# Reordering both openings of a hybrid attention and mixture-of-experts layer: the first tiles of the projection, and the indices and gathers of expert 0

## The chip, the cores and the metric

One core of a Trainium2 chip runs the whole layer as one program. The metric is the device time of one execution in microseconds. Of several executions the median is taken, and it can tell two versions of this kernel apart from about 0.2% (4.5 us) on.

## The reference

```python
h   = rmsnorm(x) @ w_in            # 1024 tokens x 1024 -> 3584 columns, float32
mix = concat(retention(h), stick_breaking_attention(h))
x   = x + mix @ w_out
xf  = rmsnorm(x)
logits = xf @ w_router + b_router            # 32 experts
top_logits, top_idx = lax.top_k(logits, 4)
top_w = softmax(top_logits)
# tokens are sorted by expert; each expert takes its own tokens
gu   = xb @ w_gate_up[e] + b_gate_up[e]      # gate and up, 2 x 1024 columns
hid  = (clip(up) + 1) * min(gate) * sigmoid(1.702 * gate)
y    = hid @ w_down[e] + b_down[e]
x    = x + sum over the 4 experts of y * weight
```

## The kernel before

The program gives each engine one instruction stream of its own, and the streams are tied by counting semaphores that the source writes out: `then_inc` raises one, `wait_ge` holds the engine's queue until it has a value. Within an engine everything runs in the written order.

**The first opening** (to the first product of the input projection). SyncE issues the first four token tiles of x (128 rows each, L506), and behind the second tile seven small vector loads (`load_vectors`, L491 to L496: the norm weights). Then come the first slab of w_in (256 columns, L501), the rope table (L511) and the second slab. ScalarE's queue issues the table of constants (L633, 666 KB), GpSimd's the router's bias and weights (L558, L559). For each tile ScalarE squares and sums (`square`, L638), takes the root (L640); VectorE inverts (L1178) and scales (L1182, `normalise`); TensorE transposes by the identity matrix in the constants (`turn_tile`, L838); VectorE multiplies by the norm weight while it takes the result out of PSUM (L1190, `to_raw`). VectorE does not begin tile 1 until the vectors are in and turned (L1206, L845). A float32 product is made of three faster ones, so each operand is split in an upper part (ScalarE, L644 for weights, L651 for tokens) and a lower part (VectorE subtracts, L1196 for a slab, L1201 for tokens). The first product (L860) needs the lower part of slab 0 and of the first two token blocks.

**The middle** is projection, retention, stick-breaking attention (L942 to L971) and the output projection with the router. There the loop at L1029 does, for tile i, `out_proj(i)` (L1005 to L1007), then `turn(i-1)` (L1018, eight transposes) and `route(i-2)` (L1026). VectorE adds the residual (L1362), ScalarE squares, roots and scales (L762, L764, L769); `turn` waits for the scaled row (`e_norm`), VectorE multiplies by the norm weight into xfT (L1375), and `best` (L1381 to L1392) picks the four experts. Output rows and scaled rows are stored by SyncE (L532, L534).

**The second opening** (from the last router product to the first product of expert 0) is one VectorE chain. `step` makes each instruction wait for the one before. It makes the softmax weights (L1427 to L1430), three bfloat16 parts of them per expert (L1432 to L1438), the position of each token in each expert's list from the rank sums that TensorE makes (L1440 to L1447), and then the list of expert 0: `list_hot` (L1453 to L1460) compares positions with 384 slots in one instruction, TensorE sums (`token_list`, L1053), `list_out` (L1465 to L1469) writes the indices. GpSimd gathers the rows (`gather`, L579 and twice L582), TensorE turns them (L1060, L1064), VectorE takes them out (`tokens_out`, L1474, L1482). Beside that, ScalarE and VectorE split the down bias (L779 to L784, L1514), VectorE clears `hid` (L1503), SyncE loads the 8 MB of expert 0's gate and up weights (L537, four chunks). Then VectorE builds a table of all list entries in 17 chained steps (`table`, L1524 to L1544), and ScalarE waits for all of it (L820) before its first sigmoid.

**The experts.** For each of 32 experts TensorE does eight blocks f of gate and up (L1119), then the down product in two halves (L1099). Block f waits until VectorE has read block f-2 out of PSUM. VectorE does per block L1567, L1569, `hidden_low` (L1556) of the block before, L1575, L1577; at f=1 the next expert's `list_hot`, at f=3 to 6 `lower` (L1551: the lower parts of the down weights), at f=4 `list_out`. The down product waits per block for the lower part of `hid` (`h_lo`) and of the weights (`c_lo`). The three streams of an expert are `block_dve` (L1558), `block_act` (L805) and `block_matmuls` (L1111).

```python
def turn(i):                       # L1011
    e.wait_ge(e_norm, i + 1)
def project(g):                    # L846
    e.wait_ge(ws_lo, u["slab"] + 1)
e.wait_ge(l_hot, 1)                # L1067
token_list()
```

## Time and profile before

| | us |
|---|---|
| median of 3 executions | 2245.34 (2244.52 to 2245.95) |
| the profiled execution's own time | 2247.83 |
| its span, first to last instruction | 2246.0 |
| TensorE busy in the span | 2148.1 (96%) |
| VectorE, ScalarE, GpSimd busy | 1282.2, 765.2, 330.6 |
| HBM traffic | 226 GB/s over the span |

The profiled execution is 2.5 us above the median, and 1.8 us of its time lie outside the span. In rows, times count from the span's start; "PE" is TensorE's products, "PEld" its weight loads, DVE VectorE, ACT ScalarE, POOL GpSimd, SP SyncE; a "q" behind a name is that engine's queue. A float32 product or its weight load in the experts shows as two records.

### The profile page before, as it was taken

The numbers are of one execution on the slowest core, as the hardware profiler recorded it, in microseconds if no ns is written. First come the engines' busy times: TensorE is split into PE (matmuls) and PEld (weight loads), VectorE is DVE, ScalarE is ACT, GpSimd is POOL, SyncE is SP. The second block draws the span as 40 slices with busy tenths as digits, with TensorE's granted clock in tenths as the row PEclk, the third lists the DMA queues.
The fourth block names the chain that finished last, engine by engine and source line by source line (L and its number), as shares of the span: only waits on it lengthen the run. The fifth ranks groups of instructions, "written<-read, shape, count | busy, mean of one in ns | idle before, by whom it ended". The sixth has DMA issues, their size and how long they took to land.

```text
span 2246.0 us, 41668 instructions
## 1 busy us (share of the span) xinstructions
PE 2148.1 (96%) x16349; PEld 1929.3 (86%) x16350; DVE 1282.2 (57%) x2579; ACT 765.2 (34%) x1360; POOL 330.6 (15%) x237
## 2 busy tenths in 40 slices
PE   6999999899969999999999999999999999999996
PEld 5888888677858999899989998999899998999996
DVE  6434534786356565456656654665566665566654
ACT  3243133576113333233333332332333333333332
POOL 1100200200000211112112111111121211212111
PEclk9999999999969999999999999999999999999998
DMA  5231221304365888678979887887798897899983
GB/s 171 79 103 57 94 94 38 113 2 151 113 213 182 287 303 309 221 247 312 324 256 314 310 296 251 289 303 254 268 315 310 309 311 255 283 313 334 331 275 95
DMA packets 257670, 510.12 MB, mean 227 GB/s; under 512 B 7450, under 2 KB 44366, under 8 KB 257294
## 3 DMA queue, kind: packets, MB, share of 16 engines
q1 hardware_dynamic: 234268, 451.96, 56.7%
q0 software_dynamic: 21968, 51.67, 9.4%
q10 hardware_dynamic: 1344, 5.14, 0.7%
q8 instruction: 75, 1.23, 0.2%
q14 instruction: 15, 0.12, 0.0%
HBM read 473.09 MB, written 33.55 MB: 226 GB/s over the span
## 4 chain that ended last, share of the span: by engine, by line
PE 93%; issue 2%; DVE 2%; DMA 1%; POOL 0%; ACT 0%; SPq 0%; ACTq 0%; DVEq 0%; POOLq 0%
PE bank L1119 45%; PE bank L1099 16%; PE bank L860 13%; PE bank L1107 3%; PE bank L958 2%; PE bank L971 2%; PE bank L1005 1%; PE bank L1006 1%; PE bank L1007 1%; PE bank L1060 1%; PE bank L1053 1%; PE bank L942 1%; PE bank L1026 1%; PE bank L1064 1%; PE bank L1084 1%
## 5 line engine op out<-in xcount | busy, mean ns | idle before, releaser
L1119 PE MATMUL bank<-hx,ring 128*128 128x140 f32 (+1 forms) x8192 | 1035.3, 289 | 21.2 <-issue 18.8
L1119 PEld LDWEIGHTS bank<-hx,ring 128*128 128x128 f32 x8192 | 1027.4, 198 | 26.0 <-issue 21.0
L1099 PE MATMUL bank<-work_r,hx_r 128*128 128x512 f32 x1024 | 335.2, 408 | 0.0
L1551 DVE TENSOR_TENSOR mix_r<-ring,work_r 128x1024 fp32r<-128x1024 f32 x256 | 305.1, 1223 | 41.1 <-ACT work_r L792 41.0
L809 ACT ACTIVATE hx<-hx 128x168 f32<-128x168 f32 x256 | 87.9, 344 | 616.1 <-DVE hx L1567 615.0
L1567 DVE TENSOR_SCALAR hx<-bank,small 128x168 f32<-128x168 f32 x256 | 100.4, 392 | 307.7 <-PE bank L1119 307.5
L792 ACT ACTIVATE work_r<-ring 128x1024 fp32r<-128x1024 f32 x256 | 257.7, 1042 | 0.0
L1099 PEld LDWEIGHTS bank<-work_r,hx_r 128*128 128x128 f32 x1024 | 188.2, 189 | 43.8 <-issue 10.4
L1099 PE MATMUL bank<-mix_r,hx_r 128*128 128x512 f32 x512 | 200.0, 391 | 0.0
L800 ACT ACTIVATE hx<-bank,small 128x512 f32<-128x512 f32 x64 | 44.0, 688 | 314.6 <-PE bank L1064 167.9
L603 POOL DMA_INDIRECT out_x<-hx,small x32 | 51.9, 1622 | 658.6 <-ACT hx L802 639.6
L579 POOL DMA_INDIRECT hx<-xn_scratch,small x33 | 33.3, 1009 | 618.7 <-DVE small L1469 618.7
L860 PE MATMUL bank<-hx_r,mix_r 128*128 128x512 f32 x480 | 114.1, 396 | 7.6 <-DVE hx_r L1201 7.6
L815 ACT ACTIVATE hx_r<-hx 128x128 fp32r<-128x128 f32 x256 | 79.0, 308 | 109.7 <-DVE hx L1577 109.7
L860 PEld LDWEIGHTS bank<-hx_r,mix_r 128*128 128x128 f32 x480 | 90.7, 190 | 27.8 <-issue 9.1
L1099 PEld LDWEIGHTS bank<-mix_r,hx_r 128*128 128x128 f32 x512 | 96.1, 188 | 21.0
L860 PE MATMUL bank<-hx_r,work_r 128*128 128x512 f32 x480 | 113.7, 394 | 0.0
L1460 DVE TENSOR_TENSOR work<-hx,cst 128x3072 bf16<-128x3072 f32 x33 | 110.6, 3352 | 0.0
L860 PEld LDWEIGHTS bank<-hx_r,work_r 128*128 128x128 f32 x480 | 89.7, 188 | 20.2 <-issue 1.9
L606 POOL DMA_INDIRECT out_x<-hx,small x64 | 100.4, 1570 | 19.5 <-issue 19.5
L1569 DVE TENSOR_SCALAR hx<-bank,small 128x168 f32<-128x168 f32 x256 | 98.2, 384 | 0.0
L1474 DVE TENSOR_TENSOR hx<-bank,small 128x512 f32<-128x512 f32 x66 | 42.6, 686 | 85.9 <-PE bank L1060 85.9
(220 smaller groups left out, 2335.6 us busy)
## 6 DMA issues: line engine op xcount, KB each, us to landing
ring<-in_w_gate_up SPq DMA_DIRECT2D x128, 2048.0 KB, 12.7
ring<-in_w_down SPq DMA_DIRECT2D x64, 2048.0 KB, 13.8
mix<-in_w_in SPq DMA_DIRECT2D x14, 1024.0 KB, 5.1
work<-in_w_in SPq DMA_DIRECT2D x14, 1024.0 KB, 5.1
ring<-in_x SPq DMA_DIRECT2D x8, 512.0 KB, 8.9
hx<-in_w_out SPq DMA_DIRECT2D x1, 4096.0 KB, 14.7
work<-in_x ACTq DMA_DIRECT2D x8, 512.0 KB, 4.7
out_x<-work SPq DMA_DIRECT2D x8, 512.0 KB, 4.4
```

The source lines that it names most:

```text
L606: e.indirect_dma_start(out=out_quarters, in_=y_o[:, r], in_offset=None, compute_op=ALU.add, out_offset=bass.IndirectOffsetOnAxis(ap=idx_sc ...
L792: e.activation(dn_hi[:, nh, k:k + 2], dn_ring[:, k:k + 2, nh * CH:(nh + 1) * CH], ACT.Copy).then_inc(c_hi, 1)
L809: e.activation(sg[:, f % 2], g1[:, f % 2], ACT.Sigmoid, scale=GALPHA).then_inc(m_sig, 1)
L815: e.activation(hid_hi[:, f], hid[:, f, 0:P], ACT.Copy).then_inc(h_hi, 1)
L860: mm = e.matmul(dst, lhs, rhs, start=k == 0 and (xs is x_hi and ws is w_hi), stop=k == KD - 1 and ws is w_lo)
L1099: mm = e.matmul(bank[2 + t][:, :], h[:, k], w[:, t, k], start=False, stop=k == KD - 1 and w is dn_lo, skip_group_check=True)
L1107: e.matmul(bank[7][quarter_rows(j), r * 2 * P:(r + 1) * 2 * P], hid[:, k, P + r * OV:P + (r + 1) * OV], dn_ring[:, k, j * 2 * P:(j + 1) * ...
L1119: mm = e.matmul(bank[f % 2][:, part * CAP:part * CAP + w], gu_ring[:, k, f * 256 + part:(f + 1) * 256:2], xT[:, k, 0:w], start=k == 0, sto ...
L1460: e.tensor_tensor(hot, pos_s.unsqueeze(2).to_broadcast([P, NT, NH * P]), slot_at.unsqueeze(1).to_broadcast([P, NT, NH * P]), ALU.is_equal) ...
L1551: e.tensor_tensor(dn_lo[:, nh, k:k + 2], dn_ring[:, k:k + 2, nh * CH:(nh + 1) * CH], dn_hi[:, nh, k:k + 2].bitcast(F32), ALU.subtract).the ...
L1567: e.tensor_scalar(g1[:, b], bank[b][:, 0:CAP], be[:, f:f + 1], GLIM, ALU.add, ALU.min)\
L1569: e.tensor_scalar(u1[:, b], bank[b][:, CAP:2 * CAP], be[:, 8 + f:9 + f], GLIM + 1.0, ALU.add, ALU.min).then_inc(m_up, 1)
```

## The change

In the first opening:

- The constants are cut: the identity (128 columns) goes first, the rest follows behind `square(1)` under the semaphore `rest_in`. The seven vectors move from SyncE's queue to ScalarE's. The router's bias and weights are issued once four tiles are squared.
- ScalarE splits slab 0 ahead of `square(3)`; the lower part of slab 0 is made by GpSimd, behind the router's loads, under a semaphore `ws_lo0` for which the first product waits.
- VectorE normalises tile 1 ahead of its wait for the vectors. TensorE turns the vectors ahead of tile 0.

In the router: `turn` transposes the unscaled row as soon as the residual is added, and `best` multiplies the sums by the inverse root in its first instruction.

In the second opening: the positions of expert 0 alone are worked out first, the compare is cut in three (`first_hot`), and two sums (`first_rows`) give the main and the overflow indices with a semaphore each (`p_idx`). The softmax weights and their parts, the positions of the other experts and the biases follow. SyncE holds chunks 2 and 3 of the gate and up weights until the gathers have landed. GpSimd clears `hid` and makes the two subtractions of the down bias, behind the gathers. The 17 table steps go between the blocks of expert 0, which becomes a copy of the VectorE block of its own, as does the last expert.

```diff
@@ sync
-                if i == 1:
-                    load_vectors()
@@
             for c in range(4):
+                if c == 2:
+                    e.wait_ge(g_in, 48)
                 e.dma_start(gu_ring[:, :, c * 512:(c + 1) * 512], gu_r[0, c]).then_inc(gu_in[c], 16)
@@ gpsimd
+            e.wait_ge(a_sq, HT)
             e.dma_start(brt, b_router.to_broadcast([P, NE])).then_inc(rt_in, 16)
             e.dma_start(wr, w_router[0].rearrange("(k p) n -> p k n", p=P)).then_inc(rt_in, 16)
+            e.wait_ge(ws_hi, 1)
+            e.tensor_tensor(w_lo[0], w_raw[0], w_hi[0].bitcast(F32), ALU.subtract).then_inc(ws_lo0, 1)
@@
-            e.wait_ge(l_ok, 1)
-            e.wait_ge(e_st[0], 128)
-            e.wait_ge(e_st[1], 128)
             e.wait_ge(e_prj, 16)
-            gather()
+            e.memset(hid, 0.0).then_inc(h_zero, 1)
+            e.wait_ge(p_idx, 1)
+            gather_main()
+            e.wait_ge(p_idx, 2)
+            gather_over()
+            e.wait_ge(g_in, 48)
+            for g in range(1, 3):
+                e.wait_ge(b_cast, g)
+                rows = slice(0, 3 * NE) if g == 1 else slice(2 * NE, 3 * NE)
+                e.tensor_tensor(b_raw[rows], b_raw[rows], bias_d[rows], ALU.subtract).then_inc(b_sub, 1)
@@ scalar
-            e.dma_start(cst[:, :], consts).then_inc(const_in, 16)
+            e.dma_start(cst[:, 0:P], consts[:, 0:P]).then_inc(const_in, 16)
+            load_vectors()
...
             for i in range(HT):
+                if i == HT - 1:
+                    upper_slab(0)
                 square(i)
-            upper_slab(0)
+                if i == 1:
+                    e.dma_start(cst[:, P:], consts[:, P:]).then_inc(rest_in, 16)
...
             e.wait_ge(sc_done, 48)
+            e.wait_ge(f_step, F_SPREAD)
             e.activation(bias_d, b_raw, ACT.Copy).then_inc(b_cast, 1)
...
-            e.wait_ge(it_step, IT_STEPS)
             with e.Fori(0, NE) as n:
                 block_act(n)
+            e.wait_ge(it_step, IT_STEPS)
@@ tensor
             def turn(i):
-                e.wait_ge(e_norm, i + 1)
+                e.wait_ge(e_x2, 2 * i + 2)
...
-            e.wait_ge(l_hot, 1)
-            token_list()
+            def first_rows(h, dst):
+                for i in range(NT):
+                    mm = e.matmul(dst, hot[:, i, h * P:(h + 1) * P], tw_s[:, i, 0:2], start=i == 0, stop=i == NT - 1)
+                return mm
+
+            e.wait_ge(p_hot, 1)
+            first_rows(0, bank[7][:, 0:2]).then_inc(p_list, 1)
+            e.wait_ge(p_hot, NH)
+            for r in range(RO):
+                mm = first_rows(1 + r, bank[6][:, 2 * r:2 * r + 2])
+            mm.then_inc(p_list, 1)
...
             mm.then_inc(bias_tr, 1)
-            e.wait_ge(bias_ok, 3)
+            e.wait_ge(l_hot, 1)
+            token_list()
             e.wait_ge(g_in, 48)
             turn_tokens()
@@ vector
-            for i in range(1, HT):
+            for i in range(2, HT):
+                to_raw(i - 2)
                 normalise(i)
-                to_raw(i - 1)
-            lower_slab(0)
+            to_raw(HT - 2)
             to_raw(HT - 1)
@@
+            step(e.tensor_scalar(f_n, f_m, -1.0, 1.0, ALU.mult, ALU.add))
+            e.tensor_copy(tw_s[:, :, 0], tile_at)
+            e.tensor_copy(tw_s[:, :, 1], tok_id[:, 0:1].to_broadcast([P, NT]))
...
+            e.wait_ge(f_rank, 1)
+            step(e.tensor_copy(f_cnt, bank[3][:, 0:NE]))
+            step(e.tensor_scalar(pos_t, tok_id, f_cnt[:, 0:1], None, ALU.add))
+            step(e.scalar_tensor_tensor(pos_t, rank[:, :, 0], -2.0, pos_t, ALU.mult, ALU.add))
+            step(e.tensor_tensor(pos_t, pos_t, f_n[:, :, 0], ALU.mult))
+            step(e.tensor_tensor(pos_s, rank[:, :, 0], pos_t, ALU.add))
+            first_hot(0)
+            first_hot(1)
+            e.wait_ge(p_list, 1)
+            step(e.tensor_reduce(l_raw[:, 0:1], bank[7][:, 0:2], X, ALU.add))
+            e.tensor_copy(idx[:, 0:1], l_raw[:, 0:1]).then_inc(p_idx, 1)
+            first_hot(2)
+            e.wait_ge(p_list, 2)
+            step(e.tensor_reduce(l_raw[:, 1:NH], bank[6][:, 0:2 * RO].rearrange("p (r c) -> p r c", c=2), X, ALU.add))
+            e.tensor_scalar(idx[:, 1:NH], l_raw[:, 1:NH], float(GR), quarter, ALU.mult, ALU.add).then_inc(p_idx, 1)
...
-            e.memset(hid, 0.0)
...
+                    if opening:
+                        table_part(f)
...
-            with e.Fori(0, NE) as n:
-                block_dve(n, n)
+            e.wait_ge(h_zero, 1)
+            block_dve(0, 0, 1, True)
+            with e.Fori(1, NE - 1) as n:
+                block_dve(n, n, n + 1)
+            block_dve(NE - 1, NE - 1)
```

## Rows read from the trace of the kernel before

**Rows 1.** The page: the chain that ended last, by engine.

```profile
PE 93%; issue 2%; DVE 2%; DMA 1%; POOL 0%; ACT 0%; SPq 0%; ACTq 0%; DVEq 0%; POOLq 0%
```

**Rows 2.** Two stretches: length, busy PE, PEld, DVE, ACT, POOL, then clock, DMA share, GB/s.

```profile
637.00:637.50 0.50, 0.50 (x3) 0.50 (x4) 0.44 (x3) 0.50 (x1) 0.00 (x0) 0.50 0.00 0
...
660.00:700.00 40.00, 30.60 (x259) 29.87 (x260) 32.70 (x66) 10.34 (x17) 3.88 (x3) 0.78 0.48 167
```

**Rows 3.** The chain of work that ended last, first opening: start, length, what.

```profile
3.89 8.11 DMA small<-in_sb_k_norm_g
...
26.07 7.26 PE bank L860 x24
```

**Rows 4.** Timeline, first opening: start, length, engine, line, tiles, [idle before <- releaser].

```profile
6.25 1.06 ACT L638 ACTIVATE ring<-ring 128x1024 f32<-128x1024 f32 x1 [3.79 <-DMA ring<-in_x]
...
11.28 1.06 ACT L638 ACTIVATE ring<-ring 128x1024 f32<-128x1024 f32 x1 [2.37 <-DMA ring<-in_x]
...
17.91 1.90 ACT L644 ACTIVATE mix_r<-mix 128x2048 fp32r<-128x2048 f32 x1
...
24.70 4.63 DVE L1201 TENSOR_TENSOR hx_r<-ring,hx_r 128x1024 fp32r<-128x1024 f32 x4 [1.12 <-ACT hx_r L651]
```

**Rows 5.** DMA issues of the first 45 us: KB each, us to landing.

```profile
small<-in_w_router POOLq DMA_DIRECT2D x1, 128.0 KB, 9.4
```

**Rows 6.** Timeline: GpSimd and VectorE side by side, first opening and attention.

```profile
35.37 2.28 DVE L1196 TENSOR_TENSOR work_r<-work,work_r 128x2048 fp32r<-128x2048 f32 x1
35.54 3.27 POOL L564 TENSOR_TENSOR ring<-ring,work 128x512 f32<-128x512 f32 x1 [32.51 <-DVE ring L1284]
...
41.56 1.30 POOL L564 TENSOR_TENSOR ring<-ring,work 128x512 f32<-128x512 f32 x1 [2.75 <-DVE ring L1284]
...
403.25 1.90 DVE L1331 TENSOR_TENSOR_SCAN work<-work,ring 128x128 f32<-128x128 f32 x4 [0.29 <-ACT work L722]
...
408.99 12.27 POOL L576 TENSOR_TENSOR ring<-ring 128x512 f32<-128x512 f32 x8 [6.12 <-DMA ring<-ring]
...
413.54 2.28 DVE L1331 TENSOR_TENSOR_SCAN work<-work,ring 128x128 f32<-128x128 f32 x2 [4.10 <-ACT work L722]
```

**Rows 7.** Line L564: all that carries it (min/median/max ns, first and last start).

```profile
L564 POOLq MODIFY_POOL_CONFIG  x2: 68/70/73, 3.0 to 3.0; - x2
```

**Rows 8.** Timeline, end of the router.

```profile
635.56 1.29 DVE L1375 TENSOR_TENSOR work<-bank,small 128x512 f32<-128x512 f32 x2
...
636.88 1.93 PE L1018 MATMUL bank<-cst,work 128*128 128x128 f32 x8 [1.19 <-DVE work L1375]
...
642.44 3.59 PE L1026 MATMUL bank<-small,work 128*128 128x32 f32 x16 [0.38 <-DVE small L1381]
```

**Rows 9.** Timeline, second opening.

```profile
648.31 0.19 DVE L1427 TENSOR_REDUCE work<-work 128x8 f32<-128x32 f32 x1 [0.36 <-ACT work L771]
...
650.25 1.88 DVE L1432 TENSOR_REDUCE work<-work 128x256 f32<-128x1024 f32 x1
...
658.47 3.35 DVE L1460 TENSOR_TENSOR work<-hx,cst 128x3072 bf16<-128x3072 f32 x1
...
663.49 1.02 POOL L579 DMA_INDIRECT hx<-xn_scratch,small  x1 [15.60 <-DVE small L1469]
...
669.95 1.94 PE L1060 MATMUL bank<-cst,hx 128*128 128x128 f32 x8 [5.21 <-DMA hx<-xn_scratch,small]
...
673.57 10.01 PE L1119 MATMUL bank<-hx,ring 128*128 128x140 f32 x64 [0.82 <-DVE hx L1482]
```

**Rows 10.** Timeline, expert 0.

```profile
683.31 1.28 ACT L809 ACT_TABLE_LOAD   x1 [11.67 <-DVE hx L1544]
...
685.06 7.90 PE L1119 MATMUL bank<-hx,ring 128*128 128x140 f32 x64 [1.48 <-DVE hx L1569]
...
701.33 0.39 DVE L1567 TENSOR_SCALAR hx<-bank,small 128x168 f32<-128x168 f32 x1
...
714.47 0.82 PE L1099 MATMUL bank<-work_r,hx_r 128*128 128x512 f32 x2
```

161 lines of the change are left out of this document (92 added, 69 removed).

## The prediction

> **What bounds the kernel now.** The page's chain first: 93% of it is TensorE [rows 1], so most of the kernel can't be moved by this change, and only the two stretches where TensorE waits for other engines count. The windows show the second of them, with 30.6 us of products in 40 at a mean clock of 0.78 [rows 2]. Then the chain in order of time. In the first opening it runs over the last of seven small vector loads, 8.1 us from its issue to its landing at 12.0, and from there over four token tiles and a slab to the first product at 26.07 [rows 3]. x tile 0 is there at 6.25, tile 1 not before 11.28 [rows 4], about when the router's weights land (issued at 2.03, plus 9.4) [rows 5]. In the second opening the chain is VectorE's from the last router product (642.44 plus 3.6) [rows 8] to the index of expert 0, then the gathers from 663.49, TensorE's turns at 669.95 and the first expert product at 673.57 [rows 9]. Past that TensorE stands until 685.06, since VectorE was building the table (ScalarE waited 11.67 us for it) [rows 10].
>
> A gain of 4.5 us (0.2%) is about what the measurement can tell from none.
>
> **First opening, part by part.** *Loads.* Without constants, vectors and router weights in front, tile 0 has the engines to itself. It landed at 6.25 while it shared them with the constants; I take 4.7 and tile 1 before 8. ScalarE's queue now issues eight small loads first, at the 0.3 to 0.4 us that SyncE took for one, so it is free at 3.7, loads its table (1.3) and squares at 5.0: 1.2 earlier than now. The vectors' last issue is at 3.7. Their landing isn't known: no sooner than about 2 us later (5.7), no later than the 8.1 of now (11.8) [rows 3]; I take 8 to 9, since they no longer queue behind a tile. TensorE turns them ahead of tile 0, and up to 9.9 that costs nothing, since VectorE normalises tile 1 meanwhile. At the bound of 11.8 the chain is 1.9 us later.
>
> *The tiles.* Tile 0 is turned from 8.8 on. VectorE takes it out at 10.9 and then needs 2.5 us per tile as now. ScalarE's slab copy (1.90) [rows 4] stands ahead of `square(3)`: 12.55 to 14.45, then `square(3)` to 15.65, for which VectorE waits about 1 us. Tile 3 is out at 19.9, ScalarE's first token copy at 20.9. The slab's subtraction on VectorE, 2.28 [rows 6], is gone from this chain.
>
> *The slab on GpSimd.* This decides the rest. It waits for the fourth square (15.65), issues both router loads (1.8), and starts at 17.5. A subtraction of 128x512 takes it 1.3 us beside a VectorE instruction that reads PSUM, so 128x2048 takes 5.2: done at 22.7. But both engines hold each other up when VectorE reads two operands from SBUF. A GpSimd instruction that began 0.17 behind such a one took 3.27 in place of 1.30; and two VectorE scans took 2.28 while GpSimd was working, where four took 1.90 before [rows 6]. So the token subtraction (1.16 each) [rows 4] that could start at 21.0 waits until 22.7, ends at 23.9, and the first product starts at 24.0. **Gain 2.1 us.** The bounds of the GpSimd instruction are 4.2 (nothing shared, a nearby kind of it took 1.04 for 512) and 13.1 (all four parts as slow as 3.27): first product at 23.0 or 30.8, a gain of 3.1 or a loss of 4.7. I take 5.2, as VectorE reads PSUM in that stretch. The Trainium skill (GPSIMD Engine Reference, Key points) says that the two share their SBUF interfaces and contend when a VectorE instruction has two SBUF inputs; the trace agrees with its 3.27.
>
> Everything behind this point is bound by TensorE and moves with it; the rest of the constants (600 KB) and slab 1 still land before 25.
>
> **The router.** For the last tile `turn` no longer waits for ScalarE's scaled row, at 636.83. But it also waits for PSUM that VectorE empties in L1375 until 636.85 [rows 8]; half the bank is free at 636.2. So only four of eight transposes come 0.6 earlier. **Gain 0.5**, and nothing in the tiles before, where TensorE has the output projection to do. The four waits that are put elsewhere (`e_tr` now ahead of the residual) are met long before. Scaling in `best` replaces an addition at the same length.
>
> **Second opening.** *Indices first.* From the last `best` at 647.7: weights' first step and f_n 0.5, two copies 0.3, rank sums at 649.2, five short steps 1.2 (650.4). The compare of 384 slots takes 3.35 [rows 9], a third of it 1.12: two thirds end at 652.7, the main index is there at 653.0, the third third at 654.2, the overflow indices at 655.3. The main gather goes out at 653.3 instead of 663.49, the two others at 655.6 and 656.9; the last takes up to 1.9 on GpSimd and lands 2 later, as now, near 660.3. *Then the rest,* VectorE alone: 1.9 to the weighted table (648.31 to 650.25). The 8.2 us from there to the compare at 658.47 [rows 9] are 4.3 for three parts of the weights, 0.4 for the copied ranks, 0.3 for f_n, 2.0 for the positions and 1.2 for expert 0's list. So 655.3 + 1.9 + 4.3 + 0.2 for a copy gives 661.6, and TensorE sums by 662.6 and can turn at once, as the gathers are there. VectorE goes on: 2.0 for the other positions, 0.4, biases 1.2, weights of expert 0 0.3: 665.5. It takes the turned tokens out in 2.0 and the first product of expert 0 starts at 667.7, not 673.57: **gain 5.9**. The bound is now VectorE, and the gathers have over 2 us to spare. Chunks 2 and 3 of the weights, held until 660.4, take the 11 us that 4 MB took before and land at about 672.5; block 4 needs them near 686. That edit costs nothing; were the gathers 13 us late it would.
>
> *What is given back.* GpSimd's bias subtraction (96x1024, 2.1 to 2.6 us at its own rate) starts when the gathers land, 660.3, in the middle of VectorE's subtractions of the weight parts, all from SBUF. By the same rows as above VectorE stands still for it: 0 if it falls on reads of PSUM, 2.6 if whole; I take **1.7 lost**. The second one falls on PSUM reads and is free. ScalarE's bias copies end near 671, before its first sigmoid at 673. Clearing `hid` (1.34 on VectorE) is done at 650 in GpSimd's idle time.
>
> *The table inside expert 0.* Its 17 steps are 9.8 us of VectorE (673.3 to 683.1). Now nothing of TensorE waits behind all of them: the stand before 685.06 (1.5) goes. But VectorE has little room. A block is 3.85 us of TensorE [rows 10]; VectorE's own part is 1.75, with a `lower` 2.98 (701.33 on). With table parts of 2.05, 1.02, 1.68, 2.05 and 1.96 blocks 2 to 6 need 3.7, 5.1, 5.3, 4.9 and 4.8, and block 1 has the compare with 4.0 before them. From a first product at S, VectorE starts block 2 at S+15.8 and block 7 at S+39.6, where TensorE has finished it at S+34.6. The down product then waits for the last `hid` parts and ends its first half at S+42.9. Now it begins the second half at 714.47 [rows 10], S+40.9. **So 2.1 are lost again**; between 0 (TensorE finds all it needs) and the whole 9.8.
>
> **The sum.** 2.1 + 0.5 + 5.9 - 1.7 - 2.1 = 4.7 us. The profiled execution would take 2243.1 instead of 2247.83, its span 2241.3; against the median of 2245.34 that is **2240.6 us**. Behind expert 0 TensorE sets the pace. The two further copies of VectorE's block are new code, but VectorE idles several us at the start of each expert: 0.
>
> **Rivals.** *A: the clock survives the router.* The granted clock is at half (1.2 GHz) from 637.0 on [rows 2], and was at full (2.4 GHz) before it, over 1.2 us of idle TensorE behind small products. The last `turn` took 1.93 and the router sums 3.5 each [rows 8], where at full clock the same take 1.04 and 1.9. The new order halves this pause. If the clock holds, 0.9 and twice 1.6 come on top: 2236.5. Against it: the work before the fall is small products in both. 15%.
>
> *B: GpSimd's subtraction holds up the first product,* and the result is slower. For it: 3.27 beside VectorE. At 13.1 us the first product starts at 30.8, 4.7 later than now, and with 2.6 from the middle the time is 2247.4. It decides from 8.5 us on (17.5 to 26.0). A configuration instruction belongs to this line's first use, at 3.0, and there the first arithmetic came 32 us later [rows 7], so what it costs was hidden, and now it would stand on the path. The Trainium skill (GPSIMD Engine Reference, Instruction dispatch) gives some 6 us for the first call of a freshly loaded kernel; by that the first product starts near 28.6 and the time would be about 2245.2. No row shows such a load. 15%.
>
> *C: VectorE stays the bound and the middle gives nothing.* Table and contention at 6.5 together cancel the 6.4 of router and indices; only the first opening's 2.1 is left: 2243.2. 15%.
>
> *D: the edits are hidden anyway,* as with late vectors (0.2 left of the first opening) and gathers slow behind weights: 2245. 5%.
>
> **Chances.** The forecast's case has 50%, with its own range 2238.5 to 2243, a little over half of it beyond 0.2%. Faster 0.28 + 0.15 + some from C = 0.45; slower by over 0.2% only from B with more behind it, 0.08; same 0.47. The range from 2235.0 to 2247.0 holds A, C and D, the ends of the GpSimd term short of its worst, and most of B.
>
> **What would show it.** First L860 near 24.0 with GpSimd's new instruction at 5.2 us ending before it. The last L1018 from near 636.3, at half clock. First gather 10 us earlier than now, landed before the sums of expert 0's weights end. The first L1119 5 us earlier. VectorE busy without a gap from block 1 to 7 of expert 0, and TensorE waiting 2 to 3 us for L1556's output. The forecast is wrong if GpSimd's subtraction exceeds 8.5 us, or if the down product of expert 0 starts its second half less than 1 us earlier than now relative to the first projection product.

## The result and the profile after

The changed kernel takes 2232.18 us (median of 4 runs, 2229.66 to 2237.12) beside 2244.93 us (median of 4 runs, 2242.77 to 2245.95) for the kernel before: a ratio of 0.9942, 95% interval 0.9926 to 0.9957. That is 12.8 us off, where 4.7 were forecast; the time lies below the range's lower end of 2235.0, on the side that had a chance of 0.45. Twice more, on other chips, the same pair gave 0.9936 (0.992 to 0.9951) and 0.9954 (0.9941 to 0.9968). The profiled execution is the longest of the four, 2237.12 us with a span of 2235.3, against a span of 2246.0 before: 10.7 us are to be found in the two traces.

**First opening.** The timeline of the changed kernel answers to the L1196, L1201 and L860 of [rows 3, 4] (start, length, engine, line, tiles, idle before and what ended it):

```profile
17.70 4.51 POOL L560 TENSOR_TENSOR mix_r<-mix,mix_r 128x2048 fp32r<-128x2048 f32 x1
...
20.34 6.36 DVE L1238 TENSOR_TENSOR hx_r<-ring,hx_r 128x1024 fp32r<-128x1024 f32 x4 [1.12 <-ACT hx_r L670]
...
23.45 2.90 PE L885 MATMUL bank<-hx_r,mix_r 128*128 128x512 f32 x6 [4.95 <-DVE hx_r L1238]
```

GpSimd's slab subtraction, the new L560, takes 4.51 us from 17.70 on. The first projection product comes at 23.45 us instead of 26.07. VectorE's four token subtractions, which begin beside GpSimd, take 6.36 us together where they took 4.63. The first product needs only the first of them (two token blocks). That one takes 2.96 us where the others take 1.21, and ends at 23.30, 1.1 us behind GpSimd's end at 22.21 (min/median/max ns of the line):

```profile
L1238 DVE TENSOR_TENSOR hx_r<-ring,hx_r x4: 1212/1213/2956, 20.3 to 25.5; 128x1024 fp32r<-128x1024 f32 x4
```

**This lead does not last in the profiled execution.** At the half turn of the projection TensorE waits 2.56 us in both kernels. Here are the 48 products behind that wait, first before, then after:

```profile
218.03 11.16 PE L860 MATMUL bank<-hx_r,mix_r 128*128 128x512 f32 x48 [2.56 <-DVE hx_r L1201]
```

```profile
216.43 12.77 PE L885 MATMUL bank<-hx_r,mix_r 128*128 128x512 f32 x48 [2.56 <-DVE hx_r L1238]
```

They take 11.16 us before and 12.77 after. The windows put this down to the granted clock, the column ahead of the last two: from 210 to 230 us it is 1.00 before and 0.91 after.

```profile
210.00:230.00 20.00, 17.44 (x99) 1.00 0.16 53
```

```profile
210.00:230.00 20.00, 17.45 (x86) 0.91 0.16 53
636.00:660.00 24.00, 12.89 (x96) 0.52 0.79 257
660.00:700.00 40.00, 33.05 (x286) 0.82 0.66 229
```

The clock from 636 to 660 us is near half level (1.2 GHz), as it was before, and from 660 to 700 us TensorE has 33.1 us of products in the place of 30.6 [rows 2].

**Second opening.** The rows that answer to those of [rows 8, 9], all engines:

```profile
645.51 0.20 DVE L1424 MAX8 small<-small 128x8 f32<-128x32 f32 x1
...
647.04 1.40 POOL L596 MEMSET hx<- 128x1536 f32 x1
...
647.19 1.40 DVE L1469 TENSOR_SCALAR work<-small 128x256 f32<-128x256 bf16 x1
...
652.77 1.75 POOL L580 DMA_INDIRECT hx<-xn_scratch,small  x1 [4.33 <-DVE small L1488]
...
659.24 2.11 POOL L605 TENSOR_TENSOR work<-work,cst 96x1024 f32<-96x1024 f32 x1 [1.87 <-DMA hx<-xn_scratch,small]
659.40 2.20 DVE L1503 CAST hx<-work 128x256 bf16<-128x256 f32 x1
...
663.58 2.12 POOL L605 TENSOR_TENSOR work<-work,cst 32x1024 f32<-32x1024 f32 x1 [2.23 <-ACT cst L806]
663.59 1.95 PE L1085 MATMUL bank<-cst,hx 128*128 128x128 f32 x8
663.68 2.30 DVE L1510 TENSOR_TENSOR work<-work 128x256 f32<-128x256 f32 x1
...
668.43 1.29 DVE L1539 TENSOR_TENSOR hx<-bank,small 128x512 f32<-128x512 f32 x2 [0.17 <-issue]
```

The last `best` has its maximum at 645.51 (646.29 before), the main gather goes out at 652.77 (663.49), TensorE turns the tokens at 663.59 (669.95), and the first expert product starts at 670.41 (673.57): 3.2 us earlier. Three VectorE rows are far too long for their size. L1469 takes 1.40 us beside GpSimd's memset, L1503 takes 2.20 and L1510 2.30, each beside one of GpSimd's bias subtractions (L605, 2.11 and 2.12). The gathers have landed by 659.24, when L605 starts, and TensorE and the tokens wait for VectorE.

**Expert 0.** VectorE runs through it almost without a gap, as forecast, but it reaches the eighth block at 707.70, 37.3 us behind the first product, where the working had 39.6. The down product's second half starts at 710.72, 40.3 us behind it (42.9 in the working, 40.9 before) and 1.1 us earlier than before against the first projection product:

```profile
706.55 1.23 DVE L1616 TENSOR_TENSOR mix_r<-ring,work_r 128x1024 fp32r<-128x1024 f32 x1
...
707.70 0.39 DVE L1632 TENSOR_SCALAR hx<-bank,small 128x168 f32<-128x168 f32 x1
...
710.51 3.50 DVE L1616 TENSOR_TENSOR mix_r<-ring,work_r 128x1024 fp32r<-128x1024 f32 x3 [0.65 <-ACT work_r L814]
...
710.72 0.39 PE L1119 MATMUL bank<-cst,small 96*128 96x512 bf16 x1
```

**The jump back to the loop's head.** Now for the part that the prediction had no term for. At the head of five experts (the one behind expert 0, and each one behind an expert of the 168-wide form) TensorE stands still for "issue": it waits for nothing that the profile shows. The other 26 jumps back show no idle time. One of the five, before and after:

```profile
1571.56 0.72 PE L1099 MATMUL bank<-work_r,hx_r 128*128 128x512 f32 x2
1572.13 0.40 PE L1099 MATMUL bank<-mix_r,hx_r 128*128 128x512 f32 x1
1576.66 5.73 PE L1119 MATMUL bank<-hx,ring 128*128 128x140 f32 x23 [4.13 <-issue]
```

```profile
1564.66 0.72 PE L1134 MATMUL bank<-work_r,hx_r 128*128 128x512 f32 x2
1565.23 0.40 PE L1134 MATMUL bank<-mix_r,hx_r 128*128 128x512 f32 x1
1568.38 6.83 PE L1154 MATMUL bank<-hx,ring 128*128 128x140 f32 x41 [2.75 <-issue]
```

It is 4.13 us before and 2.75 after. The five add up to 18.85 us (3.00, 3.12, 4.31, 4.13, 4.29) before and 14.47 (2.85, 2.56, 3.26, 2.75, 3.05) after. The DMA view shows what moves meanwhile besides weights: queue 8 brings instructions in packets of 16 KB, and two of them come around the end of the last product (1572.52 before, 1565.63 after). Here is each in a window of half a microsecond (queue and kind: packets, MB, share of 16 engines). Before, 1570.9 to 1571.4 and 1571.5 to 1572.0:

```profile
q8 instruction: 1, 0.02, 15.3%
q8 instruction: 1, 0.02, 28.4%
```

After, 1562.8 to 1563.3 and 1564.5 to 1565.0:

```profile
q8 instruction: 1, 0.02, 11.1%
q8 instruction: 1, 0.02, 12.9%
```

A share times 16 engines and 0.5 us is the time of the packet. Before, the two start 0.5 us apart, the second takes 2.3 us and has landed at 1573.96. After, they start 1.7 us apart, the second takes 1.0 us and has landed at 1565.74. The next product starts 2.7 and 2.6 us behind that landing.

So the 10.7 us of the two spans are: 3.2 at the first expert product, 0.7 in expert 0 (54.4 us from its first product to that of expert 1, first stall included, 55.1 before), 4.2 in the four further stalls, and 2.4 in the 128 products right behind the second and the fourth one, which took 21.39 and 18.34 us before and 20.11 and 17.19 after. There the clock came up again sooner: from 4 to 6 us behind the stall its mean is 0.52 and 0.55 before and 1.00 both times after.

### The profile page after: what moved, and what is told of

It is laid out like the page before. It is cut to its first block, busy times and chain, and to the rows that moved or that the text cites. A ratio compares the mean times of both kernels' runs of the same rounds, so it can differ in the third digit from the quotient of the medians.

```text
span 2235.3 us, 41581 instructions
## 1 busy us (share of the span) xinstructions
PE 2147.6 (96%) x16373; PEld 1927.7 (86%) x16374; DVE 1279.5 (57%) x2579; ACT 765.4 (34%) x1360; POOL 341.8 (15%) x241
## 4 chain that ended last, share of the span: by engine, by line
PE 67%; issue 1%; DVE 1%; POOL 0%; ACT 0%; ACTq 0%; POOLq 0%; DVEq 0%
PE bank L1154 45%; PE bank L1134 16%; PE bank L1142 3%; PE bank L1085 1%; PE bank L1078 1%; PE bank L1119 1%; PE bank L1089 1%; PE bank L1125 0%; DVE work L1525 0%; POOL out_x L615 0%; DVE hx L1632 0%; ACT hx L831 0%; DVE hx L1640 0%; DVE hx L1642 0%; DVE mix_r L1616 0%
## 5 line engine op out<-in xcount | busy, mean ns | idle before, releaser
L1154 PEld LDWEIGHTS bank<-hx,ring 128*128 128x128 f32 x8192 | 1024.6, 198 | 23.1 <-issue 21.1
L615 POOL DMA_INDIRECT out_x<-hx,small x64 | 100.6, 1572 | 19.5 <-issue 19.5
L1642 DVE SCALAR_TENSOR_TENSOR hx<-hx 128x168 f32<-128x168 f32 x256 | 85.3, 333 | 8.9
## 6 DMA issues: line engine op xcount, KB each, us to landing
ring<-in_w_gate_up SPq DMA_DIRECT2D x128, 2048.0 KB, 12.6
```

Source lines behind the costliest of these rows:

```text
L615: e.indirect_dma_start(out=out_quarters, in_=y_o[:, r], in_offset=None, compute_op=ALU.add, out_offset=bass.IndirectOffsetOnAxis(ap=idx_sc ...
L1154: mm = e.matmul(bank[f % 2][:, part * CAP:part * CAP + w], gu_ring[:, k, f * 256 + part:(f + 1) * 256:2], xT[:, k, 0:w], start=k == 0, sto ...
L1642: e.scalar_tensor_tensor(hid[:, f, 0:CAP], u1[:, b], 1.0 - GLIM, gs[:, b], ALU.max, ALU.mult)\
```

## The experiments

Three theories stood for the unforecast part. **Placement:** where the loop's code lies in TensorE's stream of instructions sets the length of the stalls; the change adds 24 small products ahead of the loop and so shifts it. **Openings:** the stalls and the rest follow from the earlier starts, through transfers and the clock. **Chance:** their length is luck. Each run gives a ratio to the kernel before on the same chip, with its 95% interval.

### The changed kernel again

No edit, twice: `c_after` and, beside the last experiment, `c_after2`.

> The changed kernel once more, as the yardstick for what follows. Placement theory (the stalls of TensorE at its jump back to the head of the expert loop depend on where the loop's code lies in the instruction blocks): the five stalls at the loop-back (after expert 0 and after each expert of the 168-wide form) sum to 13.5 to 15.5 us again, against 18.9 in the kernel before. Chance theory (their length is luck of each execution): the sum moves by 2 us or more. In both the ratio is 0.993 to 0.996. The lead of the first opening, lost at the half turn of the projection in the trace at hand (1.6 us at 210 us, none at 226 us), is kept here if the clock's level after that pause is luck, and lost again if it is the rule.

> The changed kernel, beside the next run on one chip. Ratio 0.993 to 0.9945, stalls 14 to 15.5 us, first expert product 25 us behind the last best-of-32.

Measured: 0.9936 (0.992 to 0.9951) and 0.9954 (0.9941 to 0.9968); stalls 14.92 and 14.72 us; first expert product 25.0 and 24.9 us behind the start of the last maximum (L1424), as in the first trace (24.9). Chance is out. The half turn's products took 12.59 and 12.48 us from 215.44 and 215.79 on, so they end 1.2 and 0.9 us ahead of those of the kernel before: a part of the first opening's lead was lost in both, not all of it as in the first trace.

### One opening alone

`e1_first` is the kernel before with the loads, the token tiles and GpSimd's slab of the change; `e2_second` is the change with those undone.

> The kernel before with the first opening of the change alone. Placement theory: the stream of TensorE has as many instructions as before, so the five loop-back stalls stay at 18 to 19.5 us and only the start gains: first projection product at 23.4 us, at most 2.6 us off the time, less 1.6 if the clock stays at half level after the half turn: ratio 0.9988 to 0.9995. Rival (the whole time follows from earlier starts and what they do to the clock): over 4 us off, ratio under 0.998.

> The change without its first opening: router and second opening alone. Placement theory: 24 matmuls more than before ahead of the expert loop, so the loop-back stalls are 13.5 to 15.5 us; with 3.2 us at the first expert product, 0.5 within expert 0 and up to 2.3 of clock behind the stalls the time is 8 to 11 us under the kernel before, ratio 0.995 to 0.9965. Rival (the stalls depend on where the transfers stand that the openings moved): the stalls are between the two, 16 to 19 us, and the ratio is 0.9975 or more.

Measured: first opening alone 0.9990 (0.9979 to 1.0002), first product at 23.25 us, half turn 12.51, stalls 18.68 us. Second opening alone 0.9955 (0.994 to 0.997), stalls 14.82. The stalls go with the 24 added products, not with the lead. About 1 us of the first opening's 2.6 is seen at the end, and the interval includes no gain at all.

### Padding TensorE's stream

The sharp test. Tiny products that nobody reads, in a pause in which TensorE waits for the gathers, `N` of them:

```diff
             mm.then_inc(bias_tr, 1)
+            for _ in range(N):
+                e.matmul(bank[3][:, 480:482], ones_b, f_m[:, 0, 0:2], start=True, stop=True)
```

> The kernel before, with 24 tiny products more (128x2, written to a spare piece of PSUM, nobody reads them) on TensorE ahead of the expert loop, in a pause in which TensorE waits for the gathers. Nothing else differs. Placement theory: the code of the expert loop lies as far into the instruction stream as in the changed kernel, so the five loop-back stalls fall from 18.9 to 13.5 to 15.5 us and the time by 4 to 7 us, ratio 0.997 to 0.998. Rival (the stalls follow from the reordered openings, by the state of transfers and clock): stalls 18 to 19.5 us and a ratio of 0.9995 to 1.0010.

> The changed kernel with 24 more of the tiny products that nobody reads ahead of the expert loop (so 48 more than the kernel before has). Block theory (the stall is set by how many instruction blocks of 256 have to be fetched at the jump back, so by the position of the loop in the stream modulo 128 matmuls with their weight loads): 24 lie on one side of a step; 48 stay there or cross another one, so the five stalls are 14 to 15.5 us or 18 and more, not in between; the first is likelier: ratio 0.993 to 0.9945. Rival (each 24 products shorten them by another 4 us, without steps): 10 to 11.5 us and 4 us faster than the changed kernel.

> The changed kernel with 104 of the tiny products, 128 more than the kernel before has: with their weight loads one whole block of 256 instructions. Block theory: the loop lies within its blocks as in the kernel before, so the five stalls are 18 to 19.5 us again and the time is 4 to 7 us above the changed kernel, ratio 0.9955 to 0.9970. Rival (any lengthening helps, or it is not the position but the delay that the products add): stalls of 15.5 us or less, ratio 0.993 to 0.995.

> The kernel before with 72 of the tiny products on TensorE ahead of the expert loop. So far the five loop-back stalls are 18.9 us at 0 products more, 14.9 at 24 (in both kernels), 14.0 at 48 and 18.1 at 128. Block theory (two levels, by how many blocks the jump back has to fetch): 14 to 15.5 or 18 to 19.5 us, nothing between, and a ratio of 0.9965 to 0.998 in the first case, 0.999 to 1.001 in the second. Rival (a smooth course with its bottom near 48): 15.5 to 17.5 us.

> The kernel before with 100 of the tiny products. Block theory: 14 to 15.5 us or 18 to 19.5, nothing between; it shows on which side of 100 the step back to the level of 128 lies. Rival (smooth course): 16.5 to 18 us.

The table has the matmuls ahead of the loop over those of the kernel before (the change itself counts for 24), and the sum of TensorE's idle times of over 0.6 us put down to "issue" from expert 0 on:

| kernel | matmuls more | stalls, us | ratio (95%) |
|---|---|---|---|
| before | 0 | 18.85 | 1 |
| first opening alone | 0 | 18.68 | 0.9990 (0.9979 to 1.0002) |
| before, 24 added | 24 | 14.94 | 0.9977 (0.9968 to 0.9987) |
| after | 24 | 14.47 | 0.9942 (0.9926 to 0.9957) |
| after, 24 added | 48 | 13.95 | 0.9936 (0.9922 to 0.9949) |
| before, 72 added | 72 | 56.93 | 1.0230 (1.0214 to 1.0247) |
| before, 100 added | 100 | 17.70 | 1.0008 (0.9999 to 1.0017) |
| after, 104 added | 128 | 18.14 | 0.9966 (0.9954 to 0.9977) |

The stall that was 4.13 us before and 2.75 after, in the kernel before with 24 products added, in the changed kernel with 104 added, and in the kernel before with 72 added, where it has company:

```profile
1573.97 8.23 PE L1121 MATMUL bank<-hx,ring 128*128 128x140 f32 x43 [3.00 <-issue]
```

```profile
1568.23 6.99 PE L1156 MATMUL bank<-hx,ring 128*128 128x140 f32 x32 [4.06 <-issue]
```

```profile
1598.32 2.38 PE L1121 MATMUL bank<-hx,ring 128*128 128x140 f32 x12 [3.21 <-issue]
1602.92 2.47 PE L1121 MATMUL bank<-hx,ring 128*128 128x140 f32 x9 [2.23 <-issue]
...
1656.43 3.17 PE L1121 MATMUL bank<-hx,ring 128*128 128x140 f32 x12 [8.71 <-issue]
1661.26 2.00 PE L1121 MATMUL bank<-hx,ring 128*128 128x140 f32 x7 [1.66 <-issue]
```

**Placement is shown.** 24 products nobody reads, in the kernel before, take 3.9 us of stalls and 4.6 us of time away (2241.83 us beside 2246.46). Products that fill up the count to 128 bring the stalls of the changed kernel back to 18.14 and take about half of its gain: 2239.44 us, where the one with 24 added took 2233.21 on the same chip. From the first product of expert 1 to the end, the two profiles with no matmuls more take 1517.4 us each, the 13 with 24 take 1504.4 to 1511.4, the two with 48 take 1510.5 and 1511.7, the one with 100 takes 1514.1 and the one with 128 takes 1517.3.

The Trainium skill (Runtime: NRT & Kernel Launch, Instruction fetch mechanics) says that an engine's instructions are fetched in blocks of 16 KiB, 256 of them, ahead of need and in sequence only, and that a taken branch out of what is held waits for a fetch. The trace agrees in three points: packets of 16 KB on queue 8 (42 of them with 0.69 MB from 660 to 2200 us), a stall of 2.5 to 4.5 us at the jump, and about the same stalls at 0 and at 128 matmuls, which with their weight loads are 256 instructions.

Three expectations fell, though. There are not two levels: at 72 the loop has sixteen such idle times, some inside the experts and up to 8.71 us long, and queue 8 carries 71 packets in the place of 42. At 100 the sum is 17.70, between the two levels that the block theory allowed: the first two stalls are short (2.65 and 2.49), the other three long (4.04 to 4.45). And the step from 18.9 to 14.9 us isn't one block fetched less: the kernel before carries 42 packets with and without the 24 products.

What differs is when the two packets at the jump come. Here are the last three stalls of every profile but that of 72 (times of the earlier packet count back from the end of the last product):

| matmuls more | stalls | earlier packet asked for, us before | starts apart, us | longer packet takes, us | stall, us |
|---|---|---|---|---|---|
| 0, 100, 128 | 12 | 0.8 to 1.4 | 0.1 to 0.9 | 1.9 to 2.5 | 4.0 to 4.5 |
| 24, 48 | 45 | 2.0 to 2.8, 3.5 to 3.8 | 1.1 to 3.1 | 0.9 to 1.5 | 2.7 to 3.3 |

In the first row the two packets overlap, in the second they never do. The later packet is asked for up to 1 us before the end of the product in both. And each of the 95 stalls in these 19 profiles ends 2.6 to 3.3 us behind the landing of its last packet. So the padding moves the earlier packet clear of the later one, and that is worth about 1.2 us in each of these three stalls. Which instructions a packet holds, and what fills the time between its landing and the product, no run shows. Nor does one show why at 72 some packets are asked for as late as 5 us into a stall.

### GpSimd and VectorE in the second opening

`e8_bias_late` moves GpSimd's bias subtractions behind the turned tokens; `e9_both` also has its memset earlier; `e13_both_p24` is that with 24 tiny products more.

```diff
-            e.wait_ge(g_in, 48)
+            e.wait_ge(g_xT, 4)
             for g in range(1, 3):
                 e.wait_ge(b_cast, g)
```

```diff
+            e.wait_ge(e_prj, 16)
+            e.memset(hid, 0.0).then_inc(h_zero, 1)
             e.wait_ge(e_log, NT)
...
-            e.wait_ge(e_prj, 16)
-            e.memset(hid, 0.0).then_inc(h_zero, 1)
             e.wait_ge(p_idx, 1)
```

> The changed kernel with GpSimd's two subtractions of the down bias put behind the turned tokens of expert 0 instead of ahead of them. Contention theory (a GpSimd tensor_tensor holds up the VectorE instruction beside it for about its whole length: two casts and sums of 128x256 took 2.2 and 2.3 us instead of 0.4): VectorE's chain shortens by 3.5 to 4 us, the first expert product comes 3 to 4 us earlier against the end of the router, and the time is 3 to 4 us under the changed kernel, ratio 0.9915 to 0.993. Rival (something else sets the length of these VectorE instructions, or the gathers are late next): the first expert product moves by under 1 us and the ratio stays at 0.9935 to 0.995.

> A version that may beat both: the changed kernel with GpSimd's two bias subtractions behind the turned tokens of expert 0, and its memset of the hidden rows ahead of its wait for the last router row, where VectorE is idle, instead of beside VectorE's 128x256 step. Contention theory: that VectorE step takes 0.25 to 0.4 us instead of 1.40, the indices of expert 0 come 1.1 us earlier, and the first expert product lies 20.4 us behind the last best-of-32 instead of 25.3 (21.5 with the bias subtractions alone moved): ratio 0.9915 to 0.9930. Rival (the gathers bound the second opening once VectorE is free): the first expert product stays at 21.5 us and the ratio at that of the late subtractions, 0.9925.

> The version with GpSimd's bias subtractions late and its memset early, beside the changed kernel on one chip. If the 4 us by which its first expert product comes earlier (20.9 us behind the last best-of-32 instead of 25.0) reach the end, its ratio is 0.0015 to 0.002 under that of the changed kernel; if expert 0 gives a part back, as the first trace of it showed (55.5 us from its first product to that of expert 1, instead of 54.2), 0.001.

> The best candidate: bias subtractions late, memset early, and 24 tiny products ahead of the expert loop (48 more than before, the position with the shortest stalls so far). Block theory: the position is on the same level as without them, so 14 to 15 us of stalls and the same time as without the products, ratio 0.9915 to 0.9930. Rival (48 is better than 24 by 1 us): 13 to 14 us, ratio 0.991 to 0.992.

The three long rows of VectorE in the version with both moves, and its first expert product:

```profile
643.56 0.20 DVE L1424 MAX8 small<-small 128x8 f32<-128x32 f32 x1
...
645.25 0.29 DVE L1469 TENSOR_SCALAR work<-small 128x256 f32<-128x256 bf16 x1
...
657.14 0.39 DVE L1503 CAST hx<-work 128x256 bf16<-128x256 f32 x1
...
659.61 0.42 DVE L1510 TENSOR_TENSOR work<-work 128x256 f32<-128x256 f32 x1
...
664.46 1.98 PE L1154 MATMUL bank<-hx,ring 128*128 128x140 f32 x11 [2.19 <-DVE hx L1547]
```

L1469 takes 0.29 us instead of 1.40, L1503 0.39 instead of 2.20 and L1510 0.42 instead of 2.30. The first expert product lies 20.9 us behind the start of the last maximum, not 25.0 (21.2 with the bias moves alone: where L1469 is short, VectorE waits 0.68 us for the rank sums behind it). **The contention costs the changed kernel 4.1 us at the first expert product, shown.** A part comes back: VectorE is now the bound in expert 0, where TensorE waits 0.46 us for a pair of banks and 0.91 us for the last hidden part, and expert 0 takes 55.0 to 55.6 us instead of 54.2 to 54.8. Ratios: bias late 0.9925 (0.9912 to 0.9939), both 0.9924 (0.9912 to 0.9937), with 24 products more 0.9934 (0.992 to 0.9947, a little above what was expected; stalls 14.75, first expert product again 20.9 behind). Side by side with the changed kernel on one chip, `e9_both2` took 2230.12 us (2225.33 to 2232.99, 6 runs) and `c_after2` 2234.19 (2233.01 to 2236.68, 6 runs); the ratios are 0.9933 (0.9917 to 0.9948) and 0.9954 (0.9941 to 0.9968). The intervals overlap a little, and every run of the first is under every run of the second, if only by 0.02 us. **On this chip the version beats both kernels,** the changed one by some 4 us. Over all chips the distance is less sure: 0.9924 to 0.9934 for the versions with late bias subtractions, 0.9936 to 0.9954 for the changed kernel.

### Weights behind the gathers

`e12_no_hold`, the changed kernel without a wait:

```diff
             for c in range(4):
-                if c == 2:
-                    e.wait_ge(g_in, 48)
                 e.dma_start(gu_ring[:, :, c * 512:(c + 1) * 512], gu_r[0, c]).then_inc(gu_in[c], 16)
```

> The changed kernel without SyncE's wait for the gathers ahead of the third and fourth gate/up chunk of expert 0, so that all 8 MB are queued at once. Theory of the change (the gathers must not stand behind the weights on the same DMA engines): the three gathers land 3 to 8 us later than 657 us against the issue at 651, expert 0 waits for them again and the first expert product comes up to 5 us later: ratio 0.9945 to 0.996. Rival (VectorE's chain bounds the second opening, and half of the 4 MB have already landed at that time): the first expert product stays 25.3 us behind the last best-of-32 and the ratio at 0.993 to 0.9945.

Measured: 0.9933 (0.9921 to 0.9945). The hold is worth nothing. GpSimd's bias subtraction, which starts when the gathers have landed, starts at 661.13 us, 6.4 behind the last gather's issue, in the place of 3.1 in `c_after`. But by then VectorE is through with the parts of the weights; the subtraction holds up one instruction in their stead (a copy of 128x8, 2.09 us long), the second one falls for the most part on reads of PSUM, and the first expert product lies 23.1 us behind the last maximum instead of 25.0. The gathers came late, as the first theory said, and it did not matter, as the rival said.

### The table of expert 0

`e3_table_ahead`: the 17 steps ahead of the block again.

```diff
-            block_dve(0, 0, 1, True)
+            for f in range(KD):
+                table_part(f)
+            block_dve(0, 0, 1)
```

> The changed kernel with the 17 table steps of VectorE ahead of expert 0's block again, instead of inside it. Measure: from the first gate/up product of expert 0 to that of expert 1, 54.2 to 54.7 us in the changed kernel, 54.8 to 55.1 in the kernel before. The prediction's step (the table inside makes VectorE the bound and gives 2.1 us back): with the table ahead this stretch is 52 to 53 us and the whole about 2 us faster. Rival (the table inside is covered by TensorE; ahead of the block it delays the first gate and up sums, and TensorE waits for its second bank pair as in the kernel before, 1.5 us): 55 to 56.5 us, the whole 0.5 to 2 us slower than the changed kernel.

Measured: 0.9933 (0.9919 to 0.9948), 54.3 us from the first product of expert 0 to that of expert 1, as in the changed kernel. TensorE waits once, 0.77 us, for its second pair of banks:

```profile
678.73 7.90 PE L1154 MATMUL bank<-hx,ring 128*128 128x140 f32 x64 [0.77 <-DVE hx L1634]
```

Both expectations missed: inside or ahead, the table costs the same here, within the noise.

### The slab of the first opening

`e4_slab_dve` gives the first slab's lower part to VectorE, `e10_slab_first` leaves it with GpSimd but ahead of the two router loads:

```diff
+            e.wait_ge(ws_hi, 1)
+            e.tensor_tensor(w_lo[0], w_raw[0], w_hi[0].bitcast(F32), ALU.subtract).then_inc(ws_lo0, 1)
             e.wait_ge(a_sq, HT)
             e.dma_start(brt, b_router.to_broadcast([P, NE])).then_inc(rt_in, 16)
             e.dma_start(wr, w_router[0].rearrange("(k p) n -> p k n", p=P)).then_inc(rt_in, 16)
-            e.wait_ge(ws_hi, 1)
-            e.tensor_tensor(w_lo[0], w_raw[0], w_hi[0].bitcast(F32), ALU.subtract).then_inc(ws_lo0, 1)
```

> The changed kernel with the first slab's lower part made by VectorE ahead of the last token tile's turn, not by GpSimd. GpSimd theory (4.5 us on GpSimd, and VectorE's four token subtractions beside it take 6.4 to 6.7 instead of 4.6 us: the engines' shared access is what costs): the slab takes 2.3 us of VectorE, the token subtractions 4.6 us again, and the first projection product comes at 23.3 to 24 us, as early as with GpSimd (23.4): no difference that can be measured, but nothing gained by GpSimd either. Rival (VectorE's chain bounds this opening and GpSimd takes 2.3 us off it): first product at 25 to 26 us, 1.5 to 2.5 us slower.

> The changed kernel with GpSimd's slab subtraction ahead of the two router loads that it issues, so that it can start when the slab's upper part is there (14.1 us) instead of at 17.7 us. Theory (the first projection product waits for VectorE's first two token subtractions, which run beside GpSimd and are held up): they begin at 20.0 us with GpSimd done, the first takes 1.2 us, and the first product comes at 21.3 to 22 us instead of 23.4: 1.5 to 2 us off, if the half-level clock after the half turn does not change. Rival (VectorE's other work between 14 and 18 us is held up instead, by as much): first product at 23 to 24 us and no difference.

The early GpSimd slab and what VectorE does beside it (the helper lines are shifted by the edit):

```profile
13.81 4.49 POOL L557 TENSOR_TENSOR mix_r<-mix,mix_r 128x2048 fp32r<-128x2048 f32 x1 [13.38 <-ACT mix_r L663]
...
15.42 3.44 DVE L1219 TENSOR_SCALAR ring<-ring,small 128x1024 f32<-128x1024 f32 x1
...
22.73 4.63 DVE L1238 TENSOR_TENSOR hx_r<-ring,hx_r 128x1024 fp32r<-128x1024 f32 x4 [1.12 <-ACT hx_r L670]
...
24.10 4.18 PE L885 MATMUL bank<-hx_r,mix_r 128*128 128x512 f32 x9 [3.22 <-DVE hx_r L1238]
```

The scaling of a token tile (L1219: one tensor operand and a scalar, 128x1024) takes 3.44 us instead of 0.75, held up until GpSimd has finished; the token subtractions take 4.63 again, and the first product comes at 24.10, later than the 23.45 of the changed kernel. With the slab on VectorE (2.28 us) it comes at 23.57. Ratios 0.9935 (0.9922 to 0.9948) and 0.9942 (0.9929 to 0.9955), none to be told from the changed kernel. The first opening's gain is not GpSimd's doing: with the loads and copies in the new order, the slab may stand on either engine.

### The router's turn

`e5_turn_norm` has `turn(i)` wait for `e_norm` again instead of `e_x2`.

> The changed kernel whose router turns each tile of x2 only when ScalarE's normalised rows are there, as in the kernel before (values and everything else as in the changed kernel). Theory (the last tile's square, root and normalisation stood between the projection's end and the last turn; it is worth 0.6 us at the last best-of-32): the last router row's VectorE work starts 0.5 to 1 us later against the end of the projection, and the ratio goes up by 0.0003 at most. Rival (the turns of the last two tiles are late by the whole ScalarE chain, and the half-level clock falls earlier): 2 us or more slower.

Measured: 0.9954 (0.9941 to 0.9967). The last maximum starts 12.6 us behind the router sums of tile 5 (L1051 at 630.80), in the changed kernel 11.8 (631.89 in `c_after`): the edit is worth 0.8 us there, as the theory said. Its ratio lies above that of most other runs of the changed kernel, but not above all (0.9954 was also measured for the changed kernel itself), so more than 0.8 us isn't shown.

### What stays open about the clock

The half turn's 48 products took 11.15 to 11.17 us in 4 of the 5 profiles without the first opening's edits (before, e2, and 24 and 72 products added) and 12.72 in the fifth. Of the 15 with them, 3 have 11.16 or 11.17 and 12 have 12.48 to 12.78. What TensorE does ahead of the wait, and the wait itself (2.56 us), are the same. The slow form goes with the early start, but not always, and no run here tells why.

The end of the router has two forms as well. In 4 of the 14 profiles in which `turn` takes the unscaled row (`e2_second`, `p24_after`, `p104_after`, `e9_both2`) the last turn and the router sums behind it take some 1.6 us less than in the other ten. Here they are in the changed kernel, then in `p104_after`:

```profile
636.28 1.62 PE L1043 MATMUL bank<-cst,work 128*128 128x128 f32 x8 [0.70 <-DVE work L1414]
637.70 3.46 PE L1051 MATMUL bank<-small,work 128*128 128x32 f32 x16
```

```profile
633.33 1.16 PE L1043 MATMUL bank<-cst,work 128*128 128x128 f32 x8 [0.70 <-DVE work L1416]
634.32 2.34 PE L1051 MATMUL bank<-small,work 128*128 128x32 f32 x16
```

In none of the six profiles in which `turn` waits for `e_norm` is it so. The last router sums take 3.6 us in all of them.

## Why the prediction was wrong

**First opening, 2.1:** 2.6 in the first product. The chain was right: the first token subtraction is held up until GpSimd is done, as forecast. GpSimd's subtraction was put at 5.2 us and took 4.51. **"Everything behind this point is bound by TensorE and moves with it"** failed: in 12 of 15 profiles the half turn took 1.3 to 1.6 us back, and at the end about 1 us was seen.

**Router, 0.5:** 0.8 by undoing it. Right in kind and nearly in size. In the three profiles of the changed kernel itself the clock stayed at half and rival A did not occur. In 4 of the 14 profiles with this edit it occurred in part, 1.6 of its 4.1 us.

**Second opening, 5.9 less 1.7:** from the end of the last `best`, the working had 20.0 us to the first expert product without contention (647.7 to 667.7). With GpSimd out of the way it is 19.5 (20.9 from the start of the maximum, which is 1.4 ahead of that end). So the chain was right to 0.5 us; **the term of contention was mis-sized,** 1.7 against 4.1. "The second one falls on PSUM reads and is free" was wrong, as the second subtraction met L1510, which reads SBUF; and "clearing `hid` is done in GpSimd's idle time" overlooked that a memset holds VectorE up too (1.1 us on L1469, of which 0.3 reach the first product).

**The table, less 2.1:** expert 0 became some 0.5 us shorter (54.2 to 54.8 us in the profiles with the change's order, 54.7 to 55.3 in the five with the old one, 55.1 of them before), not 2.1 longer. The mechanism was there (VectorE without a gap, TensorE waiting 0.57 and 0.32 us for hidden parts), the size wasn't: block 2 began 15.1 us behind the first product, not 15.8, and the five blocks behind it took 22.2 us together (685.53 to 707.70), not 23.8.

**Behind expert 0, "TensorE sets the pace: 0":** this is the step that failed. The working counted what the change adds to VectorE's code and not that 24 products and their weight loads added ahead of the loop shift TensorE's. Undone by padding it is 6.2 us of the changed kernel's time (2239.44 against 2233.21), and given to the kernel before it is 4.6 us. What is left is 7.6 us (5.2 to 10.3), for which the forecast had 4.7: gains of 0.8 from the router, 2.3 (25.0 for 27.3 us) from the second opening and 0.7 from expert 0 are seen in the traces, and about 1 from the first opening. Of the 2.8 us that these leave, the interval takes in 2.4. The trace of `p104_after` shows where the whole of its own 8.4 us lies (2246.0 less 2237.6): 3.1 ahead of the first router turn (550.11 for 553.18), 2.2 from there to the last maximum, 2.3 to the first expert product, 0.8 in expert 0, and 0.1 behind it. In the first two are 1.6 us of rival A and some 0.5 us more than the 2.6 of the first opening; no edit gives the half microsecond, and the 1.6 did not come in the profiles of the changed kernel itself, so this part is luck.

**Rivals.** B did not occur: no row shows some 6 us for GpSimd's first call, the instruction took 4.51 us at once, and its configuration instructions 58 and 63 ns. C and D did not occur either, though C's contention is real.

## What to carry to other kernels

Look in the chain for idle time put down to "issue" at a loop's head, and in the DMA view for instruction packets beside it. Where both are there, count the instructions that an edit adds ahead of the loop, and pad the stream with harmless instructions in steps of some 24 before judging an edit that moves the time by under 1%: here padding alone was worth between 5 us off and 54 us more. Put GpSimd's work on SBUF, a memset too, where VectorE reads PSUM or stands idle; that a VectorE cast, copy or tensor_scalar reads only one tensor does not save it.

## What the runs showed of the hardware

- The length of TensorE's stall at a loop's jump back depends on the position of the loop's code in the stream, with a period that 0 and 128 matmuls fit (18.85 and 18.14 us for five jumps), down to 13.95 and up to 56.93 us in between.
- The stall ends 2.6 to 3.3 us behind the landing of the last 16 KB instruction packet (95 stalls). Two such packets that overlap cost each other time: the longer takes 1.9 to 2.5 us, where packets apart take 0.9 to 1.5, and the stalls are 4.0 to 4.5 us in the place of 2.7 to 3.3.
- GpSimd holds up some VectorE instructions with a single tensor operand: a cast 128x256 took 2.20 us instead of 0.39, a tensor_scalar 128x256 1.40 beside a memset instead of 0.29, a tensor_scalar 128x1024 3.44 instead of 0.75, a copy of 128x8 2.09 instead of 0.17. A reciprocal of 128x1 beside the same early slab subtraction took 0.16 as always. The Trainium skill (GPSIMD Engine Reference, Key points) says that the two contend where a VectorE instruction runs in a 2-port performance mode or has two SBUF inputs. The trace agrees with the second for L1510 (2.30 us for 0.42); for the instructions with one tensor only the first could apply, and no row here shows an instruction's mode.
- A tensor_tensor subtraction of 128x2048 took GpSimd 4.51 us in the change's place and 4.49 us in the earlier one, VectorE 2.28.
